# Expert sums of a mixture-of-experts layer: turned back on the chip, or stored as rows and gathered

## The reference

```python
logits = (t @ router_w) + router_b
top_v, top_i = lax.top_k(logits, 2)
wts = softmax(top_v)                      # two gates per token
out = sum over e of gates[:, e] * (silu(h @ w1[e]) * (h @ w3[e])) @ w2[e]
x = x + g2 * out                          # g2: one vector of 1024 per group
y = x * rsqrt(mean(x * x) + eps) * final_g
```

## Time and profile before

| what | value |
|---|---|
| median of 3 runs | 1435.12 us (1435.04 to 1439.09) |
| the profiled execution's own time | 1437.01 us |
| its span, first to last instruction | 1435.2 us |
| PE busy | 1383.2 us, 96% of the span |
| DVE, ACT, POOL busy | 370.5, 245.4, 11.4 us |
| DMA over the span | 465.84 MB, mean 325 GB/s |
| mean granted PE clock | 0.975 of full speed |

### The profile page before, as it was taken

The page is one execution under the profiler, slowest core; times in us unless marked ns, Lnnn a source line. Parts: engine busy times, 40 slices in busy tenths (PEclk is TensorE's granted clock), DMA queues, the critical chain, the costliest instruction groups (busy, mean ns, idle before and its releaser), DMA issues.

```text
span 1435.2 us, 44256 instructions
## 1 busy us (share of the span) xinstructions
PE 1383.2 (96%) x21168; PEld 990.8 (69%) x21168; DVE 370.5 (26%) x641; ACT 245.4 (17%) x340; POOL 11.4 (1%) x21
## 2 busy tenths in 40 slices
PE   5799999999989999999999999999999999999997
PEld 4789999999869766665566666666666666666665
DVE  1658554555343310111010111011012011111013
ACT  1534442333231300000000000000000000000002
POOL 0000000000000000000000000000000000000000
PEclk9899999999989699999999999999999999999998
DMA  9757578555437399998899999999999999999990
GB/s 353 305 204 294 221 292 334 215 179 191 157 119 294 118 358 405 404 379 317 348 367 391 408 378 395 413 395 366 412 393 385 404 405 366 407 407 371 398 403 34
DMA packets 65041, 465.84 MB, mean 325 GB/s; under 512 B 7332, under 2 KB 7624, under 8 KB 8920
## 3 DMA queue, kind: packets, MB, share of 16 engines
q1 hardware_dynamic: 64184, 460.69, 81.6%
q0 software_dynamic: 672, 2.27, 0.6%
HBM read 461.35 MB, written 1.57 MB: 323 GB/s over the span
## 4 chain that ended last, share of the span: by engine, by line
PE 92%; DMA 4%; ACT 2%; DVE 2%; issue 0%; SPq 0%; DVEq 0%; POOL 0%
PE ps L423 91%; DMA raw<-dense_stream 4%; ACT hT L976 1%; DVE w_lo L1095 1%; ACT w_hi L950 1%; PE ps L502 0%; PE ps L835 0%; PE ps L566 0%; DVE xT L1322 0%; ACT rnd L981 0%; SPq L875 0%; DVE xT L1404 0%; DVE hT L1184 0%; DVE arena L1389 0%; DVE ada_rows L1140 0%
## 5 line engine op out<-in xcount | busy, mean ns | idle before, releaser
L423 PE MATMUL ps<-raw,hg 128*32 128x256 f32 x10752 | 587.5, 379 | 0.0
L423 PEld LDWEIGHTS ps<-raw,hg 128*32 128x32 f32 x10752 | 347.9, 110 | 234.8 <-issue 6.7
L423 PE MATMUL ps<-rnd,w_hi 128*128 128x256 f32 x1632 | 303.2, 288 | 12.9 <-DVE rnd L1189 9.7
L423 PE MATMUL ps<-raw,arena 128*32 128x256 f32 x5376 | 296.2, 379 | 0.0
L423 PEld LDWEIGHTS ps<-rnd,w_hi 128*128 128x128 f32 x1632 | 258.1, 195 | 18.7 <-issue 11.0
L423 PEld LDWEIGHTS ps<-raw,arena 128*32 128x32 f32 x5376 | 173.8, 110 | 115.7 <-issue 1.9
L423 PE MATMUL ps<-rnd,w_lo 128*128 128x256 f32 x816 | 233.1, 286 | 0.0
L1419 DVE TENSOR_TENSOR arena<-ps,arena 64x768 f32<-64x768 f32 x48 | 46.1, 960 | 542.6 <-ACT arena L1047 542.5
L1047 ACT ACTIVATE arena<-ps 64x768 f32<-64x768 f32 x56 | 44.9, 802 | 698.7 <-PE ps L423 698.7
L423 PEld LDWEIGHTS ps<-rnd,w_lo 128*128 128x128 f32 x816 | 159.0, 195 | 0.0
L1095 DVE TENSOR_TENSOR w_lo<-raw,w_hi 128x2048 fp32r<-128x2048 f32 x53 | 121.3, 2291 | 132.4 <-ACT w_hi L950 132.4
(11 more groups left out here) (118 smaller groups left out, 388.5 us busy)
## 6 DMA issues: line engine op xcount, KB each, us to landing
raw<-moe_stream SPq DMA_DIRECT2D x336, 1024.0 KB, 7.0
raw<-dense_stream SPq DMA_DIRECT2D x101, 1024.0 KB, 7.6
out<-tok SPq DMA_DIRECT2D x4, 256.0 KB, 2.0
arena<-dft_constants POOLq DMA_DIRECT2D x1, 640.0 KB, 8.8
tok<-in_x_prompt SPq DMA_DIRECT2D x1, 512.0 KB, 6.4
tok<-in_x_sample SPq DMA_DIRECT2D x1, 512.0 KB, 7.8
arena<-bias_table POOLq DMA_DIRECT2D x1, 512.0 KB, 6.2
out<-arena POOLq DMA_DIRECT2D x2, 256.0 KB, 4.3
```

Source lines behind the costliest of these rows:

```text
L423: return pe.matmul(out, lhsT, rhs, start=first, stop=last, **kw)
```

## The change

The sums of an expert are no longer turned back by PE. SP stores `y_slot` to a DRAM tensor `y_rows` (8 experts x 288 rows x 1024), four transfers of 96 KB in runs of 1 KB for each expert, issued in the middle of the next expert's loads. DVE works out for each token the two rows that hold its two experts' sums (`place`, `row_f`, `row_idx`). After the last store GpSimd takes them by four indirect transfers of 128 rows (512 KB each). ACT multiplies the first row by its gate, DVE adds the second times its gate, multiplies by g2 as rows (`gate_row`) and adds to x as rows (`x_tok`); the last norm runs on token rows: a square with its sum on ACT, and one scaling on DVE. `x_tok` and `gate_row` are made by PE in expert 2 (`side_rows`: eight groups of four 128x128 transposes or products with a broadcast column), copied by ACT (`side_copy`).

The rows of `y_rows` that only later rounds would write are filled with zeros by GpSimd, eight transfers of 768 KB, after the new caches were stored. Ahead of `h_tokens` ACT waits for them.

The ring of the expert pieces has 14 slots: the 7 of `raw`, and 7 of `raw_2`, which lies where `rnd` and `w_lo` lay. The first two pieces of expert 0 are loaded when the last dense down product is done, in SP's queue behind dense piece 88; the next five wait until the last dense product is done. The loop of further rounds is written out twice instead of a loop.

```diff
+RING = 2 * RAW
+OWN_ROWS = ROUNDS * SLOTS
...
+EARLY = 2
...
-    w_lo = sb("w_lo", [P, STAGE, HALF], F32R)
-    with nc.sbuf_tensor("w_hi", [P, STAGE, HALF], F32R) as w_hi:
-        pass
+    with ExitStack() as rounded:
+        rnd = rounded.enter_context(nc.sbuf_tensor("rnd", [P, 4 * KT * T], F32R))
+        w_lo = rounded.enter_context(nc.sbuf_tensor("w_lo", [P, STAGE, HALF], F32R))
+        w_hi = rounded.enter_context(nc.sbuf_tensor("w_hi", [P, STAGE, HALF], F32R))
+    raw_2 = sb("raw_2", [P, RAW, HALF])
...
+    def ring_slot(i):
+        k = i % RING
+        order = (2, 3, 0, 1, 4, 5, 6)
+        return raw_2[:, order[k], :] if k < RAW else raw[:, (N_PRE + k) % RAW, :]
...
# PE
-        def spread(given, y_ready_at):
...
+        def side_rows(n):
+            b = ps[:, 6 + n % 2, :]
...
+            elif n > 1:
+                pe.wait_ge(aux_copied, n - 1)
+            g, half = n // 2 % 2, n % 2
+            for i in range(4):
+                c = 4 * half + i
+                if n < 4:
+                    last = pe.transpose(b[:, i * P:(i + 1) * P], xT[:, c, g * P:(g + 1) * P], ident)
+                else:
+                    last = mm(b[:, i * P:(i + 1) * P], mods[:, 1, 40 + c, g:g + 1].to_broadcast([P, P]), ident, True, True)
+            last.then_inc(aux_full, 1)
...
-                if spreads and q == (0 if e else 3):
-                    spread(job, job)
...
+                    if job == 2 and s in (1, 2, 3, 4) and q % 2 == 0:
+                        side_rows(2 * (s - 1) + q // 2)
...
-                    for g in range(GROUPS):
-                        for t in range(NG):
-                            c = g * T + t * P
-                            last = pe.transpose(ps[:, 6 + c // 512, c % 512:c % 512 + P],
-                                                give[:, t, g * P:(g + 1) * P], ident)
...
-        norm_sum(4)
-        norm_rows(4)
-        h_tokens(y_ready)
# SP
+            if n == LAST_DOWN + RAW + 1:
+                sp.wait_ge(*used_up[SPLIT.index(LAST_DOWN)])
+                for i in range(EARLY):
+                    sp.dma_start(ring_slot(i), moe_stream[i, 0]).then_inc(moe_full[i], 16)
+        def store_rows(job):
+            sp.wait_ge(y_out, job + 1)
+            at = job % EXPERTS * OWN_ROWS + job // EXPERTS * SLOTS
+            for j in range(STRIPS):
+                out = y_rows[at:at + SLOTS, j * QUARTER:(j + 1) * QUARTER].rearrange("(g m) n -> m g n", g=GROUPS)
+                sp.dma_start(out, y_slot[STRIP * j:STRIP * (j + 1)]).then_inc(y_stored, 16)
...
+                if job == 0 and i < RAW:
+                    sp.wait_ge(*used_up[N_SPLIT - 1])
+                elif job == 0 and i < RING:
+                    sp.wait_ge(*raw_free[N_PRE + i - RING])
                 sp.wait_ge(e_used, MOE_PIECES * job + i + 1)
...
+                if e and i == RING:
+                    store_rows(job - 1)
...
+        for g in range(NG):
+            sp.wait_ge(y_done, g + 1)
+            sp.dma_start(outs[g][0], tok[:, g, :]).then_inc(out_y, 16)
# POOL
+        pool.memset(tok[:], 0.0).then_inc(zeros_ready, 1)
+        pool.wait_ge(zeros_ready, 1)
+        for e in range(EXPERTS):
+            later = y_rows[e * OWN_ROWS + SLOTS:(e + 1) * OWN_ROWS, :].rearrange("(r p) d -> p r d", p=SLOTS)
+            pool.dma_start(later, tok[0:SLOTS]).then_inc(rows_clear, 16)
...
+        pool.wait_ge(rows_ready, 1)
+        for g in range(NG):
+            for c in range(2):
+                pool.indirect_dma_start(taken[:, g, c, :], None, y_rows,
+                                        bass.IndirectOffsetOnAxis(ap=row_idx[:, 2 * g + c:2 * g + c + 1], axis=0),
+                                        ).then_inc(got[g][c], 16)
# ACT
+            if job:
+                act.wait_ge(y_stored, 16 * STRIPS * job)
             act.activation(y_slot.rearrange("p g n -> p (g n)"), wide(0, slice(0, P)), ACT.Copy).then_inc(y_out, 1)
...
+        act.activation(table_probe[:], ones[:, 0:1], ACT.Sqrt)
+        for g in range(NG):
+            act.wait_ge(got[g][0], 16)
+            act.activation(taken[:, g, 0, :], taken[:, g, 0, :], ACT.Copy, scale=gate_1[:, g:g + 1]).then_inc(first_scaled, 1)
+        for g in range(NG):
+            act.wait_ge(x_final, g + 1)
+            act.activation(taken[:, g, 0, :], x_tok[:, g, :], ACT.Square, accum_out=sq_sum[:, g:g + 1]).then_inc(sq_done, 1)
+            act.wait_ge(ssq_ready, g + 1)
+            act.activation(var[:, g:g + 1], var[:, g:g + 1], ACT.Sqrt).then_inc(std_ready, 1)
# DVE
+        dve.wait_ge(y_stored, 16 * STRIPS * EXPERTS)
+        dve.tensor_copy(row_idx[:], row_f.rearrange("p g c -> p (g c)")).then_inc(rows_ready, 1)
+        for g in range(NG):
+            dve.wait_ge(first_scaled, g + 1)
+            dve.wait_ge(got[g][1], 16)
+            sum_ = taken[:, g, 1, :]
+            link(dve.scalar_tensor_tensor(sum_, sum_, gate_2[:, g:g + 1], taken[:, g, 0, :], ALU.mult, ALU.add))
+            link(dve.tensor_tensor(sum_, sum_, gate_row[:, g, :], ALU.mult))
+            dve.tensor_tensor(x_tok[:, g, :], x_tok[:, g, :], sum_, ALU.add).then_inc(x_final, 1)
+        dve.wait_ge(in_final, 16)
+        for g in range(NG):
+            dve.wait_ge(sq_done, 4 * KT + g + 1)
+            dve.tensor_scalar(var[:, g:g + 1], sq_sum[:, g:g + 1], 1.0 / D, EPS, ALU.mult, ALU.add).then_inc(ssq_ready, 1)
+            dve.wait_ge(std_ready, 4 + g + 1)
+            link(dve.reciprocal(rstd[:, g:g + 1], var[:, g:g + 1]))
+            dve.scalar_tensor_tensor(tok[:, g, :], x_tok[:, g, :], rstd[:, g:g + 1], final_row, ALU.mult,
+                                     ALU.mult).then_inc(y_done, 1)
```

More of the change, by code:

```diff
@@ L160 @@
 N_SPLIT = len(SPLIT)
-assert MOE_PIECES % RAW == 0 and len(MOE_PLAN) == MOE_PIECES
+LAST_DOWN = max(n for n, piece in enumerate(PLAN) if piece[0] == "w2")
+EARLY = 2
+assert MOE_PIECES % RING == 0 and len(MOE_PLAN) == MOE_PIECES
 ROWS = 4
@@ L753, in gather, with expert @@
             last.then_inc(hg_full, 1)
-        def spread(given, y_ready_at):
-            pe.wait_ge(give_copied, given)
-            pe.wait_ge(y_out, y_ready_at)
-            for i in range(2):
-                for g in range(GROUPS):
[L761 to L768, removed]
+        def side_rows(n):
+            b = ps[:, 6 + n % 2, :]
+            if n == 0:
+                pe.wait_ge(hg_even, KT)
+                pe.wait_ge(hg_odd, KT)
+                pe.wait_ge(mods_done, 2 * 12)
+            elif n > 1:
[8 more added lines that the diff above has]
+            last.then_inc(aux_full, 1)
+        def expert(job, batch, e):
             at = [0]
@@ L848, in round_of @@
             for e in range(EXPERTS):
-                expert(EXPERTS * r + e, BATCHES * r + e // BATCH, e, extra, spreads=again or e > 0)
-        round_of(0, -1, again=False)
-        spread(EXPERTS, EXPERTS)
+                expert(EXPERTS * r + e, BATCHES * r + e // BATCH, e)
+        round_of(0)
         most_here = pe.value_load(most[0:1, 0:1], min_val=0, max_val=T)
         with pe.If(most_here > SLOTS):
[L855 to L859, removed]
-        norm_sum(4)
-        norm_rows(4)
-        h_tokens(y_ready)
+            for r in range(1, ROUNDS):
+                round_of(r)
     @block.sync
@@ L896, in _ @@
         with sp.If(most_here > SLOTS):
-            with sp.Fori(1, ROUNDS) as r:
+            for r in range(1, ROUNDS):
                 for e in range(EXPERTS):
                     load_expert(EXPERTS * r + e, e)
[L900 to L905, removed]
+                store_rows(EXPERTS * r + EXPERTS - 1)
+        for g in range(NG):
+            sp.wait_ge(y_done, g + 1)
+            sp.dma_start(outs[g][0], tok[:, g, :]).then_inc(out_y, 16)
+        sp.wait_ge(out_y, 32)
     @block.gpsimd
@@ L969, in norm @@
                 split_ahead(halves_at["q"])
[L970 to L979, removed]
-                        act.wait_ge(h_ready, KT * k + c + 1)
-                        act.activation(h_r[0][:, c, :], hT[:, c, :], ACT.Copy).then_inc(h_round[1], 1)
+            l, half = k // 2, k % 2
+            for c in range(KT):
+                act.wait_ge(h_scaled, KT * k + c + 1)
+                for g in range(NG):
+                    sl = slice(g * P, (g + 1) * P)
+                    last = act.activation(hT[:, c, sl], hT[:, c, sl], ACT.Identity, scale=coef[:, k, c, g:g + 1],
+                                          bias=mods[:, l, 24 * half + c, g:g + 1])
+                last.then_inc(h_ready, 1)
+                if k < 2 and c % 2:
+                    act.wait_ge(h_ready, KT * k + c + 1)
+                    act.activation(h_r[0][:, c, :], hT[:, c, :], ACT.Copy).then_inc(h_round[1], 1)
         tokens_n = [0]
         def h_tokens():
+            act.wait_ge(rows_clear, 16 * EXPERTS)
             for q in range(4):
@@ L1073, in _ @@
         with act.If(most_here > SLOTS):
-            with act.Fori(1, ROUNDS) as r:
+            for r in range(1, ROUNDS):
                 round_of(r)
```

(15 more changed lines are left out.)

140 lines of the change are left out of this document (52 added, 88 removed).

## The result

The changed kernel takes 1427.16 us in the median of five runs (1426.41 to 1429.39), beside 1438.05 for the kernel before; the ratio is 0.993, with an interval from 0.9912 to 0.9948. That is some 10 us faster, where 17.4 were forecast; measured by the 1435.12 us from which the forecast of 1417.7 us was counted, it is 8.0. The time lies inside the stated range of 1411 to 1430 us, but outside 1412 to 1422, which had been given 0.66. The profiled execution took 1429.04 us, its span is 1427.2 us against 1435.2.

What follows compares the result with a forecast made beforehand. PE was taken to bound the experts. Experts -21.0, early pieces +0.3, zeros +0.5 and end +2.8 sum to -17.4 us, from the shown median 1435.12 to 1417.7 us; range 1411 to 1430, about 0.85.

Steps and rivals of the forecast that it cites:

- What bounds the kernel: Experts: PE alone holds the chain; 3.92 us of a 112.66 us period are not pieces, 28.7 us over the stage.
- Eight side groups: Expert 2: transposes and products added to PE, with their switches, cost 7.7 us (6.4 to 13.0).
- Can the stream follow: Experts: weights, stores and instructions need 388 GB/s; 395 and 419 were seen, so it costs nothing.
- the lead of 14 pieces: Experts: 36 us of loads ahead, which with the gather's pause lend the rest the stream needs.
- The zeros: Attention: 6.3 MB, 15 us at 419 GB/s, delay a dense piece and ACT's split; 0.5 us (0 to 6).
- The early pieces: Dense part: two expert pieces loaded ahead of a dense piece that the Fourier stage awaits; 0.3 us (0 to 1).
- The end: From PE's last piece to the end: 25.2 us (21 to 32) against 22.4, 2.8 us more.
- the head: Start of the end: y copy to 0.84, four stores landed at 4.05 (3.5 to 6), index conversion to 4.3 us.
- dear-rows rival: End: indirect transfers need 3.5 us each of GpSimd, 1423, or 5 us, 1428; chance 0.12, dearer still 0.05.
- The dense stall: Attention: the zeros hold ACT's splits for two groups of pieces, 3 to 4 us each: 1425; chance 0.08.
- The stream: Experts: loads become the bound below 388 GB/s; at 358 the end is 1490; chance 0.04.
- the returning waits: Experts: the 3.9 us freed on PE at each border turn into gaps: 1436; chance 0.03.

Runs made afterwards that it cites:

- experiment 3: The kernel before plus only the zero fill and ACT's wait for it: ratio 1.004, median 1442.29 us beside 1437.42.
- experiment 1: The changed kernel without the zero fill of later rounds' rows: ratio 0.9907, median 1421.14 us.
- experiments 7 and 8: Changed kernel, zeros moved into the dense SwiGLU, no early pieces: ratio 0.9869; the same with last stores from two queues, index conversion off the chain: 0.9863.

## Why the forecast was half right

**What bounds the kernel: right.** PE alone bounds the experts; 3.9 us of a period were not pieces, and all of it went: 108.77 us measured, 108.8 forecast. Eight side groups 7.8 us for 7.7. Over the stage -20.3 for -21.0, the 0.7 us being gaps that I had counted away with the spreads (891.3 less 869.9, 13.0 and 7.8 leaves 0.6).

**Can the stream follow: right, and the ring is not why.** The rate came to 410 GB/s and PE never waited; with 7 slots neither. I had written that the lead of 14 pieces lends the rest; nothing had to be lent. The Trainium skill's limit of about 358 GB/s ("DMA: Bandwidth & Descriptors", Specifications) is given there as half of the 716 GB/s that two cores share, so it was no limit for the one core that runs here: 412 GB/s were held for 110 us.

**The zeros: the step that failed.** I took "15 us at 419 GB/s", an even sharing, a landing at about 104, and 0.5 us (0 to 6). The mechanism was the one told, a late split with softmax work queued behind it. The term was mis-sized: it is 5.9 us by experiment 3 and 5.7 to 6.1 by the ends of the attention, so it makes up 5 to 5.5 of the 9.4 us by which the span missed its forecast. Two things can be read in the rows of the landing at 109.0 instead of 104, and no run tells them apart: the zeros alone ran at 229 to 237 GB/s (the windows 88 to 93 and 93 to 98), not at 419, the rate of the loads; and the dense pieces behind their backlog hardly moved for 5 us. After that the packet counts of the two queues were nearly equal. The Trainium skill says that inside a DMA engine the software and hardware queues are served round-robin (same page, SWDGE vs HWDGE vs iDMA); 189 against 185 packets from 108 to 113 us agree, 301 against 5 from 93 to 98 us do not. And the cover of "some 10 us" until PE uses the piece was no cover: DVE's half of the split waited for ACT's (7.52 us idle, 2.30 in experiment 1), DVE's softmax steps stood behind it, and PE waited 3.44 us for these, not for the piece.

**The early pieces: small, but mis-sized.** I took 0.3 us (0 to 1); the wait was 8.65 against 6.91 us where they were taken out. In the changed kernel itself they are hidden by something worse: PE's sum before that wait took 5.98 instead of 3.75 us, at a granted clock of 0.64 of full speed in the window 396 to 402 us, a mean of its two levels, 1.2 and 2.4 GHz; from 402 to 408 us it was 0.50, the lower one. With it the router's stage began 9.8 us late (484.9 against 475.1); between there and the first piece 2.4 us came back. Of the 7.4 us, some 6 are shown to be the zeros. How the rest divides into early pieces and clock is open, since the traces of one program differ by more (3.6 us in experiments 7 and 8).

**The end: the head was mis-sized.** Stores landed 6.15 us after PE's last piece, forecast 4.05 (3.5 to 6): the four issues took 2.0 us and the last store landed after 3.7 us instead of the 2.0 of the large output stores. In the four traces without a late store they had landed after 4.3 to 4.9 us, so the forecast had the usual case nearly right and left out the late one. The indirect transfers cost what I had taken from plain ones, 0.95 us to issue and 4.4 to 5.8 us to land, so the dear-rows rival falls. The fit of the Trainium skill (same page, Anatomy of one DMA) gives 3.2 us for 512 KB, an estimate that is too low here. From DVE's first sum to its last scaling it was 11.15 us for 11.55, and 3.0 us for 3.1 after it.

**The rivals.** The dense stall, given 0.08 and 1425, is what happened, as one split held for 5.1 us and not two groups for 3 to 4 each. The stream and the returning waits did not come. With the zeros out of the way the ratios are 0.985 to 0.991 in seven kernels, where 17.4 us are 0.988, but some of them have other edits too, and the agreement is in part luck: their end takes 25.4 to 28.0 us, up to 2.8 us more than the 25.2 forecast, and in four of them the first expert piece came 0.7 to 4.8 us earlier than in the trace before, which nothing in the forecast explains.

## What to carry to other kernels

Bulk work that needs 15 us at the best rate is not free in a stage with idle transfers if it is issued in one go. What counts is how long the next urgent transfer stands behind its backlog. So issue bulk work one piece at a time, or where no engine waits in order for a fresh transfer. Price a store by a store, not by the rate of the loads. And where a change needs a side job (zeros, copies, early loads), add that job alone to the old kernel: it is one run, and it showed here 5 to 6 us that the main gain had covered.

## Not expected of the hardware

- Stores from SBUF of 4 KB rows on 96 partitions, alone on the DMA engines: 229 to 237 GB/s with the engines busy for 80 to 97% of the time, beside 419 for loads of 8 KB rows.
- Loads issued behind a backlog of GpSimd's transfers hardly started for about 5 us (5 packets against 301, and 5 against 307 in experiment 3), and then shared by packets (185 against 189). Why they don't share at once was not tried.
- A 96 KB store lands after about 2.1 us, in 4 of 11 traces one of the last four only after 3.5 to 3.8; beside the weight stream after 5.8.
- An indirect transfer of 128 rows of 4 KB: 0.93 to 1.02 us on GpSimd, 4.3 to 6.4 us to land.
- PE's granted clock after the stall: PE was busy for 4.23 and 2.32 of the 5 us from 108 and from 113 us, and stood at 0.64 of full speed from 113 to 118 us, between its two levels, so a stall of the transfers cost a little more than itself.
